# A decode-and-prompt layer with paged caches: K steps three per projection tile, V steps beside the last five tiles, and window values with the probabilities as weights

## The reference

```python
h = rms_norm(x, norm_w) @ w_in                      # 1024 -> 4096 columns, split into q, k, v, gates, z
# sparse attention, 8 query heads on 2 kv heads: compressed blocks, 16 selected blocks of 64, window of 512
kc, vc = compressed_kv(kv_c)                        # a small two-layer network over 32-token blocks
o_cmp = softmax(q @ kc) @ vc
idx   = top_k(block importance from the compressed softmax, 16)
o_sel = softmax(q @ k_sel[idx]) @ v_sel[idx]
o_win = softmax(q @ k_win) @ v_win                  # "window" is what the title calls local
# differential attention, 8 heads: two softmaxes per head
a = softmax(q1 @ k1) - lam * softmax(q2 @ k2);  o_d = a @ v_d
y = x + concat(gated(o_cmp, o_sel, o_win), rms_norm(o_d)) * silu(z) @ w_out
```

## Time and profile before

| | |
|---|---|
| median of three runs | 878.55 us (876.24 to 885.22) |
| profiled execution, its own time | 877.62 us |
| its span | 875.8 us |
| of the span: rounds | 524 to 804 us |
| TensorE busy | 794.8 us, 91% |
| moved by DMA | 221.62 MB, mean 253 GB/s |

### The profile page before, as it was taken

One profiled execution on the slowest core, in us unless ns is written; L12 is line 12 of the kernel. 1 busy time (PEld: TensorE's weight loads), 2 busy tenths in 40 slices (PEclk: granted clock), 3 DMA queues, 4 the chain that ended last, 5 costly groups with the idle time before them and its releaser, 6 DMA issues.

```text
span 875.8 us, 14940 instructions
## 1 busy us (share of the span) xinstructions
PE 794.8 (91%) x4891; PEld 381.1 (44%) x4891; DVE 451.9 (52%) x980; ACT 189.2 (22%) x484; POOL 19.7 (2%) x38
## 2 busy tenths in 40 slices
PE   6999999899989889999999999897888877887998
PEld 2555545355343434444535673342433323335443
DVE  2133234336304537677536447765775673584923
ACT  1310020001102002222313303332342341243000
POOL 0000000000000100010002000000000000000000
PEclk9999999999999989999999977997978887997999
DMA  9986696969979697879674179995798888782011
GB/s 342 306 276 210 253 362 236 378 229 345 325 260 343 219 356 273 335 258 329 233 262 152 39 248 282 334 343 195 228 281 261 274 271 291 229 343 120 1 48 50
DMA packets 136872, 221.62 MB, mean 253 GB/s; under 512 B 17481, under 2 KB 65778, under 8 KB 135322
## 3 DMA queue, kind: packets, MB, share of 16 engines
q1 hardware_dynamic: 113930, 197.40, 65.5%
q10 hardware_dynamic: 20528, 14.27, 5.3%
q0 software_dynamic: 2336, 8.99, 3.0%
HBM read 214.72 MB, written 10.04 MB: 257 GB/s over the span
## 4 chain that ended last, share of the span: by engine, by line
PE 61%; SPq 12%; DVE 12%; DMA 9%; issue 4%; ACTq 1%; ACT 1%; DVEq 0%
PE banks L613 14%; PE banks L591 13%; SPq L383 8%; PE banks L1035 6%; PE banks L627 4%; PE banks L559 3%; DMA proj<-in_cmp_cache 3%; PE banks L848 3%; DMA ring<-in_dv_cache 2%; SPq L401 2%; DVE att L1718 2%; DMA ring<-in_dk_cache 2%; PE banks L894 2%; PE banks L878 1%; PE banks L916 1%
## 5 line engine op out<-in xcount | busy, mean ns | idle before, releaser
L613 PE MATMUL banks<-ring,xt 128*128 128x512 f32 x448 | 199.6, 599 | 0.0
L613 PEld LDWEIGHTS banks<-ring,xt 128*128 128x128 f32 x448 | 83.5, 191 | 104.4 <-issue 104.3
L1265 ACT ACTIVATE wide<-banks,att 128x128 f32<-128x128 f32 (+3 forms) x128 | 66.3, 523 | 176.4 <-DVE att L1718 166.6
L591 PE MATMUL banks<-proj,wide 128*64 128x256 f32 x896 | 101.6, 389 | 1.4 <-DMA proj<-in_cmp_cache 1.2
L848 PE MATMUL banks<-ring,small 128*32 128x512 f32 x512 | 79.9, 705 | 14.9 <-DMA ring<-in_dv_cache 12.1
L591 PEld LDWEIGHTS banks<-proj,wide 128*64 128x64 f32 x896 | 65.0, 141 | 40.6 <-DMA proj<-in_cmp_cache 7.0
L627 PE MATMUL banks<-ring,small 128*32 128x512 f32 x512 | 64.2, 616 | 16.2 <-DMA ring<-in_dk_cache 16.2
L1443 DVE TENSOR_SCALAR small<-small 128x510 f32<-128x510 f32 x8 | 3.4, 427 | 142.9 <-ACT small L1104 128.1
L1089 ACT ACTIVATE proj<-banks,x_rs 128x512 f32<-128x512 f32 x32 | 22.0, 687 | 211.0 <-PE banks L613 183.4
L894 PE MATMUL banks<-consts,wide 128*128 128x128 f32 x240 | 45.7, 318 | 18.1 <-DVE xt L1742 9.5
L878 PE MATMUL banks<-proj 32*128 32x128 f32 (+7 forms) x256 | 60.2, 551 | 0.0
(11 more groups left out here) (342 smaller groups left out, 814.2 us busy)
## 6 DMA issues: line engine op xcount, KB each, us to landing
ring<-in_dk_cache SPq DMA_DIRECT2D x256, 256.0 KB, 5.8
ring<-in_dv_cache SPq DMA_DIRECT2D x256, 256.0 KB, 4.1
proj<-in_cmp_cache SPq DMA_DIRECT2D x144, 128.0 KB, 3.7
ring<-in_w_in SPq DMA_DIRECT2D x7, 2048.0 KB, 10.2
proj<-in_cmp_cache ACTq DMA_DIRECT2D x80, 128.0 KB, 5.2
ring<-in_x_nat SPq DMA_DIRECT2D x2, 2048.0 KB
ring<-in_cmp_cache SPq DMA_DIRECT2D x32, 128.0 KB, 4.1
ring<-in_w_out SPq DMA_DIRECT2D x1, 4096.0 KB, 12.4
```

What stands on the lines that cost most here:

```text
L591: last = mm(to, w1[:, kv, half, lp, :], rows[:, kv, g, lp, :, :, :], start=lp + half == 0, stop=lp == LP - 1 and half == 1, tile_position= ...
L613: last = mm(banks[:, 3 + n % 2, :], xt[:, k, P * t:P * t + P], w_ring[:, c % 2, k, :], start=k == 0, stop=k == KC - 1)
L1265: last = A(e_slot(j, c)[:, 0:n], banks[:, 2 * (j % 2) + c, 0:n], ACT.Exp, bias=row_max[:, j % 4, c:c + 1], accum_out=row_sum[:, j % 4, c:c ...
```

## The change

- K steps: three beside each of the tiles i = 0 to 8 and the last one beside i = 9, which is two tiles earlier than before.
- The maximum, exponentials, weights and `probs_t` of the differential scores move up to i = 9 to 11, ahead of the window scores. `probs_t` gets a home of its own in `wide`, so that it needn't be in `small8`, which now holds one half of the prompt's exponentials (`e_slot`).
- Thirteen V steps stand beside the tiles: 2 at i = 11, 3 at 12, 3 at 13, 2 at 14, 3 at 15; one more stands ahead of the rounds. The other 50 are spread over rounds 0 to 58 (`v_round`), five in six rounds. The picks move to rounds 2, 12, 21, 31, 40, 50 and 60, the first one to i = 14.
- Window values: the probabilities (32 columns) are the weights now and the values (128 columns) move, with four sequences side by side in four column groups; two 128x128 turns put the result back in the old form. It stands beside i = 15.
- Loads: SP loads projection weights 6 and 7 after K load 51 and after the last K load. It issues no block of the selection ahead of V load 8; then 14 of the first half beside V loads 8 to 14, 26 beside V loads 17 to 29, and 52 of the second half after V loads 38 to 59. ACT issues 42 transfers of the first half beside the tiles: 4 `sel_fixed` and 6 blocks at i = 12, 10 at 13, 10 at 14, 12 at 15, then 26 in rounds 2 to 18 (39 before). `sel_run` loads up to four indices at once.

The diff, cut to its core:

```diff
-        probs_t = small8[:, :].rearrange("p (g n) -> p g n", g=PAGES)
+        probs_t = wide[:, 0:4096].rearrange("p (h u n) -> p h u n", h=4, u=16)
...
-            at = 1024 * (j % 4) + 512 * c
-            return wide[:, at:at + 512]
+            return wide[:, 1024 * (j % 4) + 512:1024 * (j % 4) + 1024] if c == 0 else small8[:, 512 * (j % 4):512 * (j % 4) + 512]
...
-        K_STEPS, K_TURN, K_LATE = 64, 6, (3, 2, 2)
-        V_EARLY = 4
+        K_STEPS, K_TURN, K_LATE = 64, 6, 3
+        V_EARLY, V_ROUNDS = 14, 60
...
-            before = K_TURN * 6 + sum(K_LATE[n % 3] for n in range(min(i, 12)))
-            return range(before, before + (K_LATE[i % 3] if i < 12 else 0))
+            before = K_TURN * 6 + K_LATE * i
+            return range(before, min(before + K_LATE, K_STEPS))
+
+        def v_round(v):
+
+            return (v - V_EARLY) * V_ROUNDS // (K_STEPS - V_EARLY)
+
+        def pick_round(b):
+
+            return v_round(8 * b + 8) if b < DEC - 1 else V_ROUNDS
...
+        def sel_run(eng, kind, n, end):
+
+            while n < end:
+                q, slot = n // N_TOP, SEL_FIRST + n % N_TOP
+                to = min(end - n, N_TOP - n % N_TOP, 4)
+                sel_ranked(eng, kind, q, slot, slot + to)
+                n += to
...
             for n in range(K_TURN * 6 + 4, K_STEPS):
-                if n == 49:
+                if n == 52:
                     sp.wait_ge(s("proj_ready"), 20)
                     sp.wait_ge(s("new_proj_ready"), 5)
                     load_w(6)
-                if n == 58:
-                    sp.wait_ge(s("proj_ready"), 24)
-                    sp.wait_ge(s("new_proj_ready"), 6)
-                    load_w(7)
                 load_k(n)
+            sp.wait_ge(s("proj_ready"), 24)
+            sp.wait_ge(s("new_proj_ready"), 6)
+            load_w(7)
             sp.wait_ge(s("index_ready"), 1)
 
-            def sel_load(q):
-
-                sel_ranked(sp, mybir.EngineType.SP, q, SEL_FIRST, 6)
-                sel_ranked(sp, mybir.EngineType.SP, q, 6, 10)
-                sel_ranked(sp, mybir.EngineType.SP, q, 10, SEL_LAST)
-
             for v in range(64):
+                load_v(v)
                 if v == 4:
                     sp.wait_ge(s("proj_ready"), 28)
                     sp.wait_ge(s("new_proj_ready"), 7)
-                    for b in range(2):
-                        sel_fixed(sp, mybir.EngineType.SP, b)
-                    for q in range(4):
-                        sel_load(q)
-                if v == 8:
+                if 8 <= v < 15:
+                    sel_run(sp, mybir.EngineType.SP, 38 + 2 * (v - 8), 40 + 2 * (v - 8))
+                if v == 17:
                     sp.wait_ge(s("proj_ready"), 32)
                     sp.wait_ge(s("new_proj_ready"), NCHUNK)
-                if 8 <= v < 21:
-                    sel_ranked(sp, mybir.EngineType.SP, 7, v - 6, v - 5)
-                if v == 32:
+                if 17 <= v < 30:
+                    sel_run(sp, mybir.EngineType.SP, 78 + 2 * (v - 17), 80 + 2 * (v - 17))
+                if v == 38:
                     sp.wait_ge(s("sel_tensor"), sel_step(0, "sel_valued"))
-                if 32 <= v < 58:
-                    n = 2 * (v - 32)
-                    q, slot = 12 + n // 13, SEL_FIRST + n % 13
-                    if n % 13 < 12:
-                        sel_ranked(sp, mybir.EngineType.SP, q, slot, slot + 2)
-                    else:
-                        sel_ranked(sp, mybir.EngineType.SP, q, slot, slot + 1)
-                        sel_ranked(sp, mybir.EngineType.SP, q + 1, SEL_FIRST, SEL_FIRST + 1)
-                load_v(v)
+                if 38 <= v < 60:
+                    sel_run(sp, mybir.EngineType.SP, 156 + 52 * (v - 38) // 22, 156 + 52 * (v - 37) // 22)
...
+            def win_values():
+
+                pe.wait_ge(s("win_vector"), step("win_probs_kept"))
+                pe.wait_ge(s("win_new_in"), 16 * DEC)
+                for bh in range(2):
+                    for kt in range(4):
+                        for i in range(4):
+                            last = mm(banks[32 * i:32 * i + 32, 2, 256 + P * bh:256 + P * bh + P], p_win_t[:, kt, 32 * bh:32 * bh + 32],
+                                      win_v[:, 4 * bh + i, kt, :], start=kt == 0, stop=kt == 3, tile_position=(0, 32 * i))
+                last.then_inc(s("win_tensor"), 1)
+
+            def win_turn():
+
+                pe.wait_ge(s("win_vector"), step("win_rows_kept"))
+                for bh in range(2):
+                    last = tr(banks[:, 2, P * bh:P * bh + P], win_rows[:, P * bh:P * bh + P], ident)
+                last.then_inc(s("win_tensor"), 1)
...
                 if i == 11:
+                    pe.wait_ge(s("scores_kept"), 8)
+                    pe.wait_ge(s("diff_weights"), 1)
+                    for g in range(PAGES):
+                        if g % 8 == 0 and g >= 16:
+                            pe.wait_ge(s("probs_kept"), g // 8 - 1)
+                        last = mm(banks[:, 6 + (g // 8) % 2, 64 * (g % 8):64 * (g % 8) + 64], scores[:, P * g:P * g + P], d_weights,
+                                  start=True, stop=True)
+                        if g % 8 == 7:
+                            last.then_inc(s("probs_turned"), 1)
                     pe.wait_ge(s("win_vector"), step("win_key_placed"))
                     pe.wait_ge(s("index_ready"), 1)
                     for b in range(DEC):
                         last = mm(banks[0:64, 2, :], q_nsa[:, b, :], win_kt[:, b, :], start=b == 0, stop=b == DEC - 1)
                     last.then_inc(s("win_tensor"), 1)
+                    pe.wait_ge(s("p_kc_normed"), 1)
+                    tr(banks[:, 5, 448:480], p_kc, ident[0:32, 0:32]).then_inc(s("p_kc_turned"), 1)
                     pe.wait_ge(s("normed"), 4)
                     turn_blocks("ks")
                     turn_blocks("kw")
+                    pe.wait_ge(s("probs_kept"), 4)
+                    for v in range(2):
+                        v_step(v)
...
+                        v_step(v)
                 if i == 12:
-                    pe.wait_ge(s("scores_kept"), 8)
+                    for v in range(2, 5):
+                        v_step(v)
+                    pe.wait_ge(s("new_proj_used"), 8)
...
                     for k in range(4):
                         turn_blocks(f"z{k}")
+                    for v in range(5, 8):
+                        v_step(v)
...
+                    pick(0)
                     pe.wait_ge(s("z_done"), 2 * TILES)
                     turn_blocks("z4")
                     turn_blocks("z5")
-                    pe.wait_ge(s("diff_weights"), 1)
+                    v_step(8)
...
                     turn_blocks("z6")
+                    win_values()
                     turn_blocks("z7")
-
-            def v_step(v):
...
-            pe.wait_ge(s("probs_kept"), 4)
-            for v in range(V_EARLY):
-                v_step(v)
-            pe.wait_ge(s("win_vector"), step("win_probs_kept"))
-            pe.wait_ge(s("win_new_in"), 16 * DEC)
-            for b in range(DEC):
-                for kt in range(4):
-                    last = mm(banks[:, 2, 256 + 8 * b:264 + 8 * b], win_v[:, b, kt, :], p_win_t[:, kt, 8 * b:8 * b + 8],
-                              start=kt == 0, stop=kt == 3)
-            last.then_inc(s("win_tensor"), 1)
+                    for v in range(10, V_EARLY - 1):
+                        v_step(v)
+
+            v_step(V_EARLY - 1)
+            win_turn()
...
-                if j < DUOS and j % 8 == V_EARLY:
-                    pick(j // 8)
-                if j + V_EARLY < 64:
-                    v_step(j + V_EARLY)
+                for b in range(1, DEC):
+                    if j == pick_round(b):
+                        pick(b)
+                for v in range(V_EARLY, 64):
+                    if j == v_round(v):
+                        v_step(v)
...
+                if i == 12:
+                    act.wait_ge(s("proj_ready"), 28)
+                    act.wait_ge(s("new_proj_ready"), 7)
+                    act.wait_ge(s("index_ready"), 1)
...
+                if i == 10:
+                    act.wait_ge(s("diff_max"), 1)
+                    A(scores, scores, ACT.Exp, bias=work[:, 144:145], accum_out=work[:, 145:146]).then_inc(s("diff_exps"), 1)
                 if i == 11:
+                    for h in range(4):
+                        act.wait_ge(s("probs_turned"), h + 1)
+                        A(wide[:, 1024 * h:1024 * h + 512], banks[:, 6 + h % 2, :], ACT.Copy).then_inc(s("probs_kept"), 1)
...
+                    for b in range(2):
+                        sel_fixed(act, mybir.EngineType.Activation, b)
+                    sel_run(act, mybir.EngineType.Activation, 0, 6)
...
+                    sel_run(act, mybir.EngineType.Activation, 6, 16)
...
+                    sel_run(act, mybir.EngineType.Activation, 16, 26)
...
```

(4 more changed lines are left out.)

174 lines of the change are left out of this document (82 added, 92 removed).

## The result

The change made the kernel slower by about half a per cent, where 1.6% less had been forecast:

| | median of its runs | lowest to highest | profiled execution |
|---|---|---|---|
| before | 878.77 us (20 runs) | 872.62 to 885.29 | 877.62 |
| after | 883.67 us (20 runs) | 875.46 to 892.59 | 875.46 |

A forecast was written before the change was run, and what follows sets the result against it. TensorE bounds beside the tiles, SP's issuing in the middle rounds. +14 - 11 - 11 - 4 - 2 = -14 us on the profiled 877.6 gives 863.6, forecast median 864.5 us; range 857 to 869 (0.50), 80% 853 to 879.

The forecast's parts named there:

- ahead of the first exponentials: Everything before the rounds' first exponentials: shorter window values against added V steps, new waits and low clock, +14 us.
- pick out of round 52: At round 52 the pick no longer stands ahead of the selected scores: -4 us.
- rounds 52 to the end: Rounds 52 to 67 and tail: two V steps less, tail untouched, -2 us.
- the first 25 rounds give back 11 of the 14 us: Rounds 0 to 24: -7 us to the first half's placing, -4 us from the later pick.
- to the placing of the first half -7: First rounds: three V steps less -4, page waits -2, ACT's last blocks -1 us.
- the +4 us for ACT's twelve: At i = 15 twelve ACT transfers, 10.3 us, stand ahead of the rounds' first exponentials: +4 us (2 to 6).
- New waits: Ahead of the rounds: +2 us at i = 9 to tile 27, +7 at i = 12, +4 at 15, +2 low clock.
- window values -8.7: Window values in the new form take 2.0 us plus 0.6 for turns, from 11.32: -8.7 us (-6.5 to -9.5).
- Rounds 25 to 52: First selected values to second placing: four V loads less on SP, the bound there, -11 us.
- rival 2: Gain eaten: rounds bound by something V steps merely filled; middle rounds -3, first rounds -3, 876 us (870 to 886); chance 0.27.
- Rival 4: Slower: ACT's transfers ahead of the rounds cost 1.3 us each, not 0.86; 890 us; chance 0.06.
- Rivals 1 and 3: Rival 1: ACT's issuing and new waits cost little, 852 to 855, chance 0.17; 3: transfers bound rounds, 860, no own chance.

The follow-up runs named there:

- Experiments 6 to 9: Changed kernel with V steps 10-12 behind tile 31: 1.0130; no V step in rounds 0-3: 1.0207; ACT's last twelve transfers spread: 1.0049; latter two: 1.0023 of before.
- experiment 3: Changed kernel with the window values back in the old form: 894.31 us, 1.0183 of the kernel before.
- experiment 2: Kernel before with only the window values in the new form: 875.58 us, 0.9986 of the kernel before.
- c_swap: Changed kernel with the 16 window scores ahead of the product for probs_t: 876.88 us, 0.9997 of the kernel before.
- a_spfirst: Changed kernel with SP instead of ACT issuing slot 12's ten transfers, ahead of V load 4: 876.63 us, 0.9966 of the kernel before.
- c_all: Changed kernel with window scores ahead of the product, SP issuing slot 12's ten transfers, V steps 10 to 12 behind tile 31: 869.52 us, 0.9904 of before.
- d_comb: Changed kernel with window scores ahead of the product, SP issuing slot 12's ten transfers, ACT's last twelve spread over rounds: 870.74 us, 0.9907 of before.
- Experiments 9 and 12: Changed kernel with ACT's last twelve transfers spread, no V step in rounds 0-3: 1.0023 of before; also SP's second list from V load 34: 1.0108.
- a_again: The changed kernel unchanged, measured and profiled a second time: 884.28 us, 1.0073 of the kernel before.

## Why the prediction was wrong

Against the profiled execution the sum said -14 us, and -2.1 came. By its own steps, with what the first profile of after measured:

| step | predicted | measured |
|---|---|---|
| ahead of the first exponentials | +14 | +16.2 (526.28 to 542.48) |
| from there to the end of the first selected values | -11 | -1.8 |
| to the second placing | -11 | -12.4 |
| pick out of round 52 | -4 | -4.7 |
| rounds 52 to the end | -2 | +0.6 |

- **The failing step is "the first 25 rounds give back 11 of the 14 us"**: 9.2 of the 11.9 us. In it the pick's part held: from the first placing to the end of the selected values are 21.8 us, where 25.7 had been (-3.9, forecast -4), and the pick waits 0.71 us in place of 3.89. What failed is "to the placing of the first half -7": from the first exponentials to that placing are 70.7 us (542.48 to 613.18), where 68.6 had been (526.28 to 594.92), so +2.1. It counted V steps, waits for pages and ACT's last blocks as if the first rounds began as before, with a filled ring and at the clock of before.
- **What the trace has in its place**: from the first exponentials to round 4 are 11.7 us and not 8.0. (The other 6.5 of the 10.2 us that rounds 0 to 4 grew by lie ahead of the first exponentials and so in the table's first row.) The waits for pages grew instead of going: 6.1 us at V steps 14 and 15 alone, where all of them were 2.8. The clock was 0.51 in rounds 0 to 4 and 0.79 in rounds 4 to 16 (0.82 and 0.88), so PE was busy as long with ten V steps as with twelve. And SP's list beside these rounds got slower, 4.4 us for a V load in place of 3.5; the prediction asked after SP's pace for the middle rounds only. How the missing gain of rounds 4 to 16 divides between clock and SP no experiment separates: PE waits there for pages 1.0 us in the first profile and 3.5 in the second.
- **Why the rounds begin badly**: V steps 10 to 13 directly ahead leave the ring empty, and twelve transfers hold ACT's exponentials at the same time. Experiments 6 to 9 show that neither mend alone brings back the 8.6 us; the +4 us for ACT's twelve was added to a sum that put the refill at nothing. The row that had the refill's cover is in the earlier trace rows: 11.32 us of window values behind four V steps. Taking them out was priced at 8.7 us. That is about right where nothing needs the cover (10 us in the changed kernel, experiment 3); where the four V steps stand ahead of them it is 1.2 us (experiment 2), and that the new order leaves the ring without cover wasn't counted.
- **New waits**: right in place (product 2.24, third turned block 6.90 us), and +2 and +7 fit their length. The low clock stood in the sum with 2 us behind the 7 us wait, and behind the 2 us wait with nothing; there the product and the window scores lose 6.5 to 8.2 us in eight of ten profiles. This is most of what made the median 8 us worse than the profiled execution, and `c_swap` recovers 7.4 us. With the wait of 6.90 us and its follow-up, removed in `a_spfirst` for 1.1%, the two are more than the whole loss against the kernel before: without both, and with a third edit that gave nothing by itself, the changed kernel takes 0.990 of it (`c_all`, `d_comb`).
- **K steps 0, V steps 0.9 each beside tiles, window values -8.7**: right (PE waits 0.5 us for K pages from 311 to 450 us; V steps take 1.92 us for two and 2.78 for three; window values 1.96 and their turn 0.44 us).
- **Rounds 25 to 52**: right for the reason given. From SP's first pair (635.72) to the last one (738.49) are 102.8 us, and DVE waits 6.09 us for blocks at the placing, so SP's list is the bound. Experiments 9 and 12 add that it matters when it starts, and what stands in SP's queue around its first wait.
- **Rounds 52 to the end**: -2 forecast, +0.6 measured; the selected scores alone take 6.14 us in place of 4.68, behind a wait of 4.27 us.
- **Rivals**: the gain was eaten (rival 2, 870 to 886 us), but only half by its mechanism: the middle rounds gave their 11 us, and the first ones, which it saw at -3, gave nothing before the placing. Rival 4's place, ACT's transfers ahead of the rounds, was right and its price not: twelve in 9.83 us is 0.82 each, not 1.3. Rivals 1 and 3 expected 852 to 855 and 860 us; against rival 3 (transfers bound the rounds), the middle rounds became shorter by SP's four loads while the DMA share fell from 0.85 to 0.79.
- **Left open**: why the clock holds in two of ten executions at the same wait; what a full ring alone would give at the rounds' start; and what sets the pace of rounds 4 to 16, clock or SP's list.

## What to carry over

Before a long piece of work is shortened or moved, ask which refills and which other queues run under it, and price the edit with that cover gone; where two things hold the same point, removing one can show next to nothing (rounds 0 to 4: 18.3 us for 18.8), so take both away before calling one innocent, and look whether the work has only moved. A wait of 2 us on a busy TensorE can cost three times its length in clock behind it, and work that needs nothing late, put ahead of the waiting instruction, is the cheapest mend. In a queue that works in order, look at what stands behind a wait: the wait at the head of the same list of transfers held SP 2.1 us behind V load 38 and 16.0 us behind V load 34.

## What the runs showed of the hardware

- A wait of 2.24 us after a long busy stretch was followed by a granted clock of 0.70 over 23 us (1.00 over the first 17 in an execution where it held), and whether it fell differs between executions of one program: 7.33 or 11.74 us for the same 64 records. The 12 runs of `a_again` spread over 12.1 us, the 12 of `c_swap`, without that wait, over 8.1; the kernel before, without it too, over 12.7 in 20 runs, so the spread alone shows little.
- ACT's activations stand still while its queue issues transfers: twelve of 32 KB took 9.83 us, and exponentials whose input was ready at 535.8 us began at 542.48.
- 64 records of 128 columns behind 32-column weights in four column groups took 1.96 us; 64 of 8 columns behind 128-column weights took 11.32.
